# Reordering the projections of a recurrent layer: v ahead of the LoRA products, shift by subtraction, channel parameters loaded during the norm

## The reference, cut to what matters

```
xx = h_shift - h                      # each quarter of the channels shifted another way, zero at the border
xr, xw, xk, xv, xa, xg = [h + xx * mu[j] for j in range(6)]
r = xr @ wr ; k = xk @ wk ; v = xv @ wv                 # 1024 x 1024 each
w_lora = tanh(xw @ w1)                # 1024 -> 64, two directions
a_lora = xa @ a1                      # 1024 -> 64, two directions
g_lora = sigmoid(xg @ g1)             # 1024 -> 160, grid tokens only
```

## Time and profile before

| | us |
|---|---|
| median of 3 runs | 4351.2 (4344.81 to 4356.38) |
| the profiled execution | 4352.07 |
| its span in the profile | 4350.3 |
| mean granted TensorE clock, share of full | 0.915 |
| TensorE matmul busy | 3608.8 (83%) |
| VectorE busy | 1254.8 (29%) |
| ScalarE busy | 779.1 (18%) |
| GpSimd busy | 619.4 (14%) |
| first DMA issue of the projections | at 1505.53 |
| last matmul of the projections | starts at 1819.9 |

### The profile page before, as it was taken

The page is one execution under the profiler, slowest core; times in us unless marked ns, Lnnn a source line. Parts: engine busy times, 40 slices in busy tenths (PEclk is TensorE's granted clock), DMA queues, the critical chain, the costliest instruction groups (busy, mean ns, idle before and its releaser), DMA issues. The chain is left out here.

```text
span 4350.3 us, 104061 instructions
## 1 busy us (share of the span) xinstructions
PE 3608.8 (83%) x46088; PEld 2318.8 (53%) x46088; DVE 1254.8 (29%) x2935; ACT 779.1 (18%) x1781; POOL 619.4 (14%) x794
## 2 busy tenths in 40 slices
PE   4999994999995189878888887769999919987787
PEld 2445543655553045467777777345656504464464
DVE  2131114111110530055555554531111130161253
ACT  1011001000000100143333332010000010151152
POOL 0000000111110100054444442001111110000000
PEclk7999995999998599889999999879999959998988
DMA  7741104999998422200000000369999933201010
GB/s 272 286 165 39 73 20 177 354 386 391 386 384 300 121 86 77 71 15 16 18 20 18 18 18 12 113 245 394 395 387 389 375 139 96 87 9 65 24 40 25
DMA packets 303038, 707.10 MB, mean 163 GB/s; under 512 B 26829, under 2 KB 50349, under 8 KB 301964
## 3 DMA queue, kind: packets, MB, share of 16 engines
q1 hardware_dynamic: 268036, 613.55, 38.3%
q0 software_dynamic: 25840, 71.67, 5.0%
q10 hardware_dynamic: 8728, 15.34, 0.9%
HBM read 648.20 MB, written 52.31 MB: 161 GB/s over the span
## 5 line engine op out<-in xcount | busy, mean ns | idle before, releaser
L901 PE MATMUL banks<-w_gate_up_ring,x_turned 128*32 128x256 f32 x12288 | 694.7, 382 | 37.1 <-DMA w_gate_up_ring<-in_moe_w_up_dram 35.6
L901 PEld LDWEIGHTS banks<-w_gate_up_ring,x_turned 128*32 128x32 f32 x12288 | 431.2, 110 | 273.8 <-issue 61.2
L919 PE MATMUL banks<-w_down_ring,hidden_turned 128*32 128x256 f32 x6144 | 344.8, 380 | 0.0
L977 DVE TENSOR_TENSOR hidden<-silu_gate,banks 128x128 f32<-128x128 f32 x192 | 55.2, 287 | 773.8 <-ACT silu_gate L957 737.8
L878 POOL DMA_DIRECT2D y_rows<-y_out_rows x256 | 141.5, 560 | 950.4 <-ACT y_out_rows L963 915.4
L919 PEld LDWEIGHTS banks<-w_down_ring,hidden_turned 128*32 128x32 f32 x6144 | 193.7, 110 | 128.1 <-issue 0.2
L337 PE MATMUL banks<-const_cols,h_tokens 128*128 128x128 f32 x240 | 54.4, 407 | 247.9 <-DVE h_tokens L310 162.2
L1914 DVE TENSOR_TENSOR inverse_both_ways<-banks,inverse_both_ways 128x512 f32<-128x512 f32 (+1 forms) x240 | 152.1, 637 | 253.1 <-PE banks L1823 252.2
L866 POOL DMA_INDIRECT x_rows<-h_rows,cell_index x64 | 62.7, 980 | 914.0 <-POOLq L42 887.7
L456 PE MATMUL banks<-gmlp_weights,h_turned_gmlp 128*128 128x512 f32 x384 | 174.9, 611 | 12.0 <-DMA gmlp_weights<-in_ga_w_in_dram 12.0
L337 PEld LDWEIGHTS banks<-const_cols,h_tokens 128*128 128x128 f32 x240 | 45.7, 217 | 257.3 <-DVE h_tokens L310 169.8
(11 more groups left out here) (457 smaller groups left out, 5336.9 us busy)
## 6 DMA issues: line engine op xcount, KB each, us to landing
w_gate_up_ring<-in_moe_w_gate_dram SPq DMA_DIRECT2D x70, 2048.0 KB, 8.8
w_gate_up_ring<-in_moe_w_up_dram SPq DMA_DIRECT2D x70, 2048.0 KB, 24.0
w_down_ring<-in_moe_w_down_dram SPq DMA_DIRECT2D x70, 2048.0 KB, 16.6
u_channels<-in_ada_w_dram SPq DMA_DIRECT2D x40, 1024.0 KB, 6.9
y_rows<-y_out_rows POOLq DMA_DIRECT2D x256, 96.0 KB
gmlp_weights<-in_ga_w_in_dram SPq DMA_DIRECT2D x8, 2048.0 KB, 8.3
ab_weights<-in_ab_w_in_dram SPq DMA_DIRECT2D x6, 2048.0 KB, 8.5
ada_first<-in_ada_w_dram SPq DMA_DIRECT2D x2, 4096.0 KB, 17.6
```

The costliest lines, as they stand in the source:

```text
L901: last = pe.matmul(ps[strip(j), GU + g, 0:2 * FQ].rearrange("p (a c) -> p a c", a=2), xT[:, e % 2, k, strip(g)], wgu[:, e % 2, :, k, j * F ...
L919: last = pe.matmul(ps[strip(j), Y + g // 2, (g % 2) * DQ:(g % 2 + 1) * DQ], hT[:, g, strip(k)], wd[:, e % 2, k, j * DQ:(j + 1) * DQ], star ...
```

## The change

The semaphore of the channel parameters moves out of `projections` into `rwkv`, under a new name of an ordinary semaphore, and SP issues their six DMAs in the norm, behind the spread rows. In `projections` SP issues the first two halves of the wide weights first, then the LoRA weights and g1, then `x_parked`. VectorE writes `xx` by eight subtractions, and the elements at the border, where the shift brings zero, by eight negations. The mixes come in the order v, w, a, g, r, k. TensorE runs the 12 sums of v first, the very first one k slice by k slice as the mix becomes ready, then the small products (w and a in banks 4 to 7, g in banks 0 and 1), waits for their evacuation, and runs r and k. ScalarE follows the same order. The diff, cut to its core:

```diff
@@ rwkv
+        (params_in,) = held.enter_context(signals(nc, "vectors_in"))
+
+        def load_params(sp):
+            with nc.allow_non_contiguous_dma(reason="vectors laid out by channel on partitions"):
+                col = lambda ap: ap.rearrange("a (k p) -> p a k", p=P)
+                sp.dma_start(params[:, 0:6, :], col(ins["rw_mu"][0])).then_inc(params_in, 16)
+                sp.dma_start(params[:, 6:8, :], col(ins["rw_w0"][0])).then_inc(params_in, 16)
...
-                      [mod_row(core, layer, t >= NT, 0) for t in range(NTA)], 1e-6, hT)
+                      [mod_row(core, layer, t >= NT, 0) for t in range(NTA)], 1e-6, hT, loads=load_params)
@@ projections
-        MIXES = [1, 4, 5, 3, 0, 2]
+        MIXES = [3, 1, 4, 5, 0, 2]
...
-            @block.gpsimd
-            def _(pool):
...
-                    pool.dma_start(params[:, 0:6, :], col(ins["rw_mu"][0])).then_inc(params_in, 16)
...
             @block.sync
             def _(sp):
+                load_wide(0)
+                load_wide(1)
                 for z in range(DIRS):
                     sp.dma_start(w1[:, :, z * LORA:(z + 1) * LORA], ...).then_inc(small_in, 16)
                     sp.dma_start(a1[:, :, z * LORA:(z + 1) * LORA], ...).then_inc(small_in, 16)
                 sp.dma_start(g1[:, :, :], ...).then_inc(small_in, 16)
+                sp.dma_start(x_parked.rearrange("(t p) d -> p t d", p=P), core.x[:, 0:NT, :]).then_inc(x_stored, 16)
+                for n in range(2, len(WIDE)):
+                    sp.wait_ge(product, ends[n - 2])
+                    load_wide(n)
                 sp.wait_ge(x_stored, 16)
@@ scalar
                 for i, (kind, n, m, half) in enumerate(SUMS):
+                    if i == 2 * NTA:
+                        for which, dst in enumerate((tw, ta)):
...
+                        act.wait_ge(lora_sum, 6)
+                        act.activation(tg[:, :], ps[:, 0, :], ACT.Sigmoid).then_inc(lora_done, 1)
+                        act.activation(tg2[:, :], ps[0:GLORA - P, 1, :], ACT.Sigmoid).then_inc(lora_done, 1)
@@ vector
-                do(dve.tensor_scalar(xx[:, :, :], hT[:, :, :], -1.0, None, ALU.mult))
...
-                    add(one(xx, 0)[:, :, 1:], one(hT, 0)[:, :, :-1])
-                    add(one(xx, 2)[:, :, :-1], one(hT, 2)[:, :, 1:])
-                add(xx[:, 4:6, GRID_W:T], hT[:, 4:6, 0:T - GRID_W])
...
+                    less(one(xx, 0)[:, :, 1:], one(hT, 0)[:, :, :-1], one(hT, 0)[:, :, 1:])
+                    minus(one(xx, 0)[:, :, 0:1], one(hT, 0)[:, :, 0:1])
+                    less(one(xx, 2)[:, :, :-1], one(hT, 2)[:, :, 1:], one(hT, 2)[:, :, :-1])
+                    minus(one(xx, 2)[:, :, GRID_W - 1:], one(hT, 2)[:, :, GRID_W - 1:])
+                less(xx[:, 4:6, GRID_W:T], hT[:, 4:6, 0:T - GRID_W], hT[:, 4:6, GRID_W:T])
+                minus(xx[:, 4:6, 0:GRID_W], hT[:, 4:6, 0:GRID_W])
...
                 for n, mu in enumerate(MIXES):
                     if n == 2:
-                        dve.wait_ge(lora_sum, 2)
-                    if n == 3:
-                        dve.wait_ge(lora_sum, 4)
-                    if n == 4:
-                        dve.wait_ge(lora_sum, 6)
-                    if n == 5:
                         dve.wait_ge(product, 2 * NTA)
+                    if n >= 3:
+                        dve.wait_ge(lora_sum, 2 * (n - 2))
@@ tensor
+                def loras():
+                    pe.wait_ge(small_in, 80)
+                    for n, w in enumerate((w1, a1)):
+                        pe.wait_ge(mix_ready, KD * (n + 2))
...
+                    pe.wait_ge(mix_ready, KD * 4)
+                    pe.wait_ge(moved, 10)
...
+                    pe.wait_ge(lora_done, 6)
+
                 for i, (kind, n, m, half) in enumerate(SUMS):
-                    j = {"v": 3, "r": 4, "k": 5}[kind]
-                    pe.wait_ge(mix_ready, KD * (j + 1))
+                    if i == 2 * NTA:
+                        pe.wait_ge(moved, 8)
+                        loras()
+                    if i:
+                        pe.wait_ge(mix_ready, KD * {"v": 1, "r": 5, "k": 6}[kind])
                     pe.wait_ge(w_in[n % 2], 16 * (n // 2 + 1))
                     if i >= 8:
                         pe.wait_ge(moved, i - 7)
                     for k in range(KD):
+                        if i == 0:
+                            pe.wait_ge(mix_ready, k + 1)
```

More of the change, by code:

```diff
@@ L1207, in projections @@
         g1 = sb("lora_g1", [P, KD, GLORA])
[L1208 to L1209 removed]
+        s = held.enter_context(signals(nc, "small_in w_in0 w_in1 xx_ready mix_ready lora_sum lora_done product moved stored0 stored1 stored2 stored3 dve_chain x_stored", core.soft))
+        small_in, w_in0, w_in1, xx_ready, mix_ready, lora_sum, lora_done, product, moved, st0, st1, st2, st3, chain_s, x_stored = s
         w_in, stored = [w_in0, w_in1], [st0, st1, st2, st3]
         WIDE = [("rw_wv", 0), ("rw_wv", 1), ("rw_wr", 0), ("rw_wr", 1), ("rw_wk", 0), ("rw_wk", 1)]
[L1213 removed]
+        MIXES = [3, 1, 4, 5, 0, 2]
         SUMS = [("v", n, t, 0) for n in range(2) for t in range(NTA)]
@@ L1219, in projections, with load_wide @@
         with nc.Block() as block:
-            @block.gpsimd
-            def _(pool):
-                with nc.allow_non_contiguous_dma(reason="vectors laid out by channel on partitions"):
-                    col = lambda ap: ap.rearrange("a (k p) -> p a k", p=P)
-                    pool.dma_start(params[:, 0:6, :], col(ins["rw_mu"][0])).then_inc(params_in, 16)
[L1225 to L1230, removed]
             @block.sync
             def _(sp):
+                ends = [max(i for i, g in enumerate(SUMS) if g[1] == n) + 1 for n in range(len(WIDE))]
+                def load_wide(n):
+                    name, half = WIDE[n]
+                    sp.dma_start(wring[:, n % 2, :, :], ins[name][0].rearrange("(k p) n -> p k n", p=P)[:, :, half * HALF:(half + 1) * HALF]).then_inc(w_in[n % 2], 16)
+                load_wide(0)
+                load_wide(1)
                 for z in range(DIRS):
@@ L1250, in _ @@
             def _(act):
[L1251 to L1257, removed]
-                for i, (kind, n, m, half) in enumerate(SUMS):
+                for i, (kind, n, m, half) in enumerate(SUMS):
+                    if i == 2 * NTA:
+                        for which, dst in enumerate((tw, ta)):
+                            for part in range(2):
+                                act.wait_ge(lora_sum, 2 * which + part + 1)
+                                act.activation(dst[:, part * HT2:(part + 1) * HT2], ps[:, 4 + 2 * which + part, 0:HT2], (ACT.Tanh, ACT.Copy)[which]).then_inc(lora_done, 1)
+                        act.wait_ge(lora_sum, 6)
+                        act.activation(tg[:, :], ps[:, 0, :], ACT.Sigmoid).then_inc(lora_done, 1)
+                        act.activation(tg2[:, :], ps[0:GLORA - P, 1, :], ACT.Sigmoid).then_inc(lora_done, 1)
                     act.wait_ge(product, i + 1)
@@ L1327, in _ @@
                     for k in range(KD):
+                        if i == 0:
+                            pe.wait_ge(mix_ready, k + 1)
                         if kind == "v":
-                            last = pe.matmul(ps[:, i % 8, :], mix[:, 1, k, m * P:(m + 1) * P], wring[:, n % 2, k, :], start=k == 0, stop=k == KD - 1)
+                            last = pe.matmul(ps[:, i % 8, :], mix[:, 0, k, m * P:(m + 1) * P], wring[:, n % 2, k, :], start=k == 0, stop=k == KD - 1)
                         else:
-                            last = pe.matmul(ps[:, i % 8, 0:HT2], wring[:, n % 2, k, m * P:(m + 1) * P], mix[:, j % 2, k, half * HT2:(half + 1) * HT2],
+                            last = pe.matmul(ps[:, i % 8, 0:HT2], wring[:, n % 2, k, m * P:(m + 1) * P], mix[:, 0 if kind == "r" else 1, k, half * HT2:(half + 1) * HT2],
                                              start=k == 0, stop=k == KD - 1)
```

43 lines of the change are left out of this document (23 added, 20 removed).

## The result

The changed kernel takes 4322.84 us in the median of 5 runs (4318.47 to 4326.33), the kernel before 4347.47 (5 runs, 4341.93 to 4356.38): ratio 0.9938, with a 95% interval of 0.9922 to 0.9954. The profiled execution took 4318.47, its span 4316.7.

A forecast was written before the change was run, and what follows sets the result against it. Stages run one after another; TensorE's wait for parameters, then eight mixes, bounds the projections' start, matmul columns the rest. Minus 19.4 plus 0.4 gives minus 19.0 us: 4332.2 from a median of 4351.2, range 4324 to 4344.

The forecast's parts named there:

- The start of TensorE: Projections: the first v product starts at 1514.8 instead of 1534.16, 19.4 us earlier, with weights and first mix arriving together.
- The slow clock at the start: First matmuls of the projections: TensorE starts at 1.2 GHz, costing about 2.7 us both before and after the change.
- The parameters: Loads on SP in the norm: 832 elements per DMA engine at 11.3 ns, 9.4 us, done by 1494.
- (a): SP in the norm: parameters become the late thing from 52 ns per element; 4357 us at the far end, chance 0.05.
- (b): SP in the norm: 30 to 50 ns per element ends the block late; gain 2 to 18 us, middle 4341, chance 0.13.
- The spread rows: Norm: these rows sit ahead of the new parameter packets in the same queue; cost nothing, at worst 1 us.
- The seams: Projections behind v: mixes for a, g, r and k stay hidden under running products; no cost.
- rival (c): Seam behind v: the a mix or a wait for evacuations shows; one full mix is 7.6 us, 4340, chance 0.05.
- The sigmoids: Projections ahead of r: TensorE waits 1.15 us for the gate's two sigmoids, as it did ahead of v.
- The exit: Semaphore clearing behind the layer costs 0.35 us, at most 1.46; queue reset at the projections' exit taken as 0.
- The sum: Whole kernel: minus 19.4 plus 0.4 gives minus 19.0 us, all of which reaches the end.
- the fourth rival: Whole kernel: the forecast itself, 4332 give or take 4 for run-to-run spread and the clock's start, chance 0.77.

The follow-up runs named there:

- early_weights: The changed kernel with both halves of the v weights loaded in the norm, behind the parameters; 4332.47 us, ratio 0.9953.
- params_more: The changed kernel with six more loads of the 6144 mixing parameters into an unused spare tile, on SP in the norm; 4327.1 us, a single run.
- the kernels with the products: Kernels before and changed, plus four unused matmul instructions (two products) ahead of the last attention; 4345.86 us before, 4325.35 changed.
- after_again: The changed kernel run again without further edits; its profiled execution took 4322.56 us.
- each part alone: Against the kernel before: only the new order of products, 4341.56 us; only the parameters moved to the norm, 4334.98 us.
- before: The kernel before the change, unedited, as first profiled; its profiled execution took 4352.07 us.
- aa_before: The kernel before, unedited, timed against itself and profiled again on another chip; 4352.34 us, ratio 1.0014.

## Why the prediction was right in its steps and wrong in its range

**The start of TensorE** (forecast 9.2 us into the stage): 8.77. The shift and its borders end 7.5 after they start, where 6.73 + 1.2 was counted; a border instruction of 8 columns takes 0.17 by itself, but the next one starts 0.08 behind it, so 0.15 was too much for most. The largest border has 128 elements per partition (0.22 us), not the 256 that were counted. Weights and mix were called a tie; the mix ends the wait, by `early_weights`. TensorE starts 19.9 earlier within the stage, against 19.4.

**The slow clock at the start** (2.7 us, the same before and after): the stretch at 0.51 lasts 4.44 us, so 2.2 are lost. The stage as a whole gained 20.2, 0.4 more than the start, about what the shorter slow stretch gives back.

**The parameters** (11.3 ns an element, taken from the router's packets): in the stretch from 1478 to 1480 the hardware queue of the kernel after shows 133.6% of 16 engines for 4589 packets, so 9.3 ns each, and the last issue is off SP at 1484.4, 14 us before the norm's last evacuation. The elements are through by about 1487 (179 packets from 1486 to 1490), where 1494 was counted. The other price of the range, 27.9 ns of the earlier trace rows, is a mixed one: some 1,100 of that stretch's packets have 512 bytes or more.

```profile
q1 hardware_dynamic: 4589, 0.03, 133.6%
```

The Trainium skill (DMA: Bandwidth & Descriptors, Bandwidth) has a floor of about 10.5 ns per packet, from the busy span of a 4 KB load issued from GpSimd, and does not say whether the packets of one engine or of all are meant. Taken as one engine's, as the prediction does, it is an elapsed time, and what answers to it is the 10.0 ns between elements in `params_more`, not the 8.9 that one takes: the two agree within 5%. The rivals (a) and (b) fall here by their own numbers; their mechanism is the one that `params_more` brings out. SP was held 7.00 us in its second parameter issue and had the time.

**The spread rows** (nothing, at worst 1 us): VectorE waits 0.56 for them in the norm, and the norm is longer by 0.1 to 0.5 in pairs of traces. **The seams** (nothing): nothing; rival (c) falls. **The sigmoids** (1.15): 1.15. **The exit** (0.35 for one more block of semaphore clearing, 0 for GpSimd's reset): timelines of the kernel after, the layer's last instruction and the next stage's first, answering to the earlier trace rows, and the end of the projections:

```profile
2809.45 0.69 DVE L2150 TENSOR_TENSOR x_tokens<-x_tokens,v_here 128x512 f32<-128x512 f32 x1
2811.92 0.80 SPq L267 DMA_DIRECT2D spread_rows<-mods  x2
```

```profile
1795.14 0.33 ACTq L1274 DMA_DIRECT2D k_channels<-proj_out  x1
1798.53 0.34 SPq L1379 DMA_DIRECT2D scan_masks<-in_scan_const_dram  x1
```

From 2810.14 to 2811.92 is 1.78, where it was 1.46: +0.32. From the last store's issue to the next stage is 3.39, where it was 3.38: the reset costs nothing.

**The sum** was -19.0; the touched stages give -20.2 + 0.5 + 0.3 = -19.4 in the first pair of profiles and -20.8 + 0.4 + 0.3 = -20.1 in the second, in the middle -19.8. This part stands.

**What failed is one term of the fourth rival's sentence and of the range: "4332 give or take 4 for the run-to-run spread and the clock's start".** It was set from three runs of one kernel and one profile, and it was too small. The stages that the change leaves alone move by more: the recurrence between 888.6 and 897.8 in the traces of this study, the experts of the first mixture between 673.8 and 679.2, the recurrent layer's output between 117.7 and 124.6, the last attention at 185 or 194. Single runs have a standard deviation of 6.3 us in the kernel before (106 runs) and of 7.5 in the changed one (29); sets of runs of the one have medians from 4347 to 4352, of the other from 4323 to 4330. From these deviations a median of five scatters by about 4 us and the reference of three by 4.5, together 6, an estimate (1.25 times the deviation over the root of the number of runs).

The miss of 9.4 us (4332.2 to 4322.84) splits so: 0.8 by the steps (19.8 for 19.0), 1.4 by the reference, which lay high (4351.2 against a mean of 4349.8), 4.8 by the first five runs of the changed kernel, which lay low (4322.84 against a mean of 4327.6), and 2.4 that are left, with a standard error of 1.5.

So most of the miss is the luck of the runs: of three later medians of the same kernel, 4323.61, 4325.18 and 4330.35, two lie inside the range.

Between the kernels with the products 1.2 are left, with 1.3. All that lies outside the norm and the projections takes 3998.0 us in the mean of the four profiles of the kernel before, with and without the products, and 3995.5 in the fourteen of changed kernels; the 2.5 between them have a standard error of 3.0. What these last one or two microseconds are stays open: chance covers them, and a small effect of the change on later stages isn't excluded. Another reading fell, that the last attention stage explains the whole surplus: with it held at 184, single runs of one kernel still differ by up to 18.6 us, and the profiled execution of `after_again` had the long stage (193.5) and took only 4322.56.

## What to carry to other kernels

Ask of a hole which wait ends last, then which would end last without it: here the parameters hid the mixes, and the mixes hide the weights; each part alone gave 7 and 11 us, and the next thing worth doing was to cut the mix. Moving the weights alone gave nothing; the cut mix was run only with the weights moved as well, and its first product, 2.47 us into the stage, comes before weights issued there would land (8.7 us or more). A load of single numbers belongs where its queue and the issuing engine have nothing due, and it stays free only until the issues outlast the block. On a kernel whose untouched stages wander by several microseconds, judge a part of 2 to 7 us by its stage in the trace, and give the whole a range taken from the scatter of several sets of runs, not of three runs.

## What the hardware showed that was not expected

- Single fp32 numbers on SP's queue take 9.3 ns each on their DMA engine (8.9 in `params_more`, one every 10.0 ns), less than the 16- and 128-byte packets' 11.3.
- TensorE, fully busy, can stay at 1.2 GHz for 27 us behind a hole of 3.3 us (8.8 us lost), or for 7, in two executions of one kernel (`before` and `aa_before`). None of five profiles with two unused products in the hole shows the long form.
